# A two-block transformer step in split fp32: the order of the work inside the attention slots, at the front of the second block's first layer, and in its output projections

## The reference, cut to what matters

```python
def first_block(x, ...):                       # one layer
    h = rms_norm(x, norm1_g)
    glu_in, q, k, v, gate_logits = split(h @ w_in)
    a = a_val * sigmoid(a_gate)
    a = silu(rms_norm(causal_depthwise_conv(a, conv_w, conv_b), conv_norm_g))   # 31 taps
    y_a = a @ w_conv_out
    q = rms_norm(q per head) * 64 ** -0.5;  k = rms_norm(k per head)
    o = dilated_window_attention(q, k, v, slopes, ((128, 1), (512, 4), (2048, 16)), mixed by log-sum-exp)
    x = x + (g_a * y_a + g_b * (o @ w_attn_out)) @ w_out       # g = sigmoid(gate_logits + gate_b)
    u = causal_depthwise_conv(rms_norm(x, norm2_g) @ w_up, ffn_conv_w, ffn_conv_b)
    return x + (silu(u_gate) * u_val) @ w_down

def second_block(x, ...):                      # layer a, then layer b
    # a: rope on q and k; an index score selects the 128 best keys of each query; softmax attention over them
    score = einsum(relu(einsum(rope(qi), rope(ki))), wi);  idx = top_k(score, 128)
    y = (softmax_attention(rope(q), rope(k), v, idx) * silu(g)) @ w_out_a
    x = layer_norm(ALPHA * x + y, ln_g[0], ln_b[0])
    # b: stick-breaking attention, no rope
    z = einsum(q, k) * 64 ** -0.5;  before = key < query
    a = exp(log_sigmoid(z) + reverse exclusive cumsum of where(before, log_sigmoid(-z), 0)), 0 elsewhere
    y = ((a @ v) * silu(g)) @ w_out_b
    return layer_norm(ALPHA * x + y, ln_g[1], ln_b[1])
```

## Time and profile before

| | |
|---|---|
| median of 3 runs | 1641.57 us |
| profiled execution | 1639.73 us, span 1637.9 us |
| TensorE (PE) busy | 1516.7 us, 93% of the span |
| VectorE (DVE) busy | 1119.3 us, 68% |
| ScalarE (ACT) busy | 744.4 us, 45% |
| GpSimd (POOL) busy | 365.0 us, 22% |
| mean granted clock of TensorE | 0.968 of full speed |

### The profile page before, as it was taken

The page is one execution under the profiler, slowest core; times in us unless marked ns, Lnnn a source line. Parts: engine busy times, 40 slices in busy tenths (PEclk is TensorE's granted clock), DMA queues, the critical chain, the costliest instruction groups (busy, mean ns, idle before and its releaser), DMA issues.

```text
span 1637.9 us, 19428 instructions
## 1 busy us (share of the span) xinstructions
PE 1516.7 (93%) x6990; PEld 1253.5 (77%) x6990; DVE 1119.3 (68%) x2092; ACT 744.4 (45%) x1464; POOL 365.0 (22%) x293
## 2 busy tenths in 40 slices
PE   8898998889999999999999989978897989999988
PEld 7677887677878788888888777867776868788766
DVE  6836679788955557547737447958787363888966
ACT  6455543556353434334424424345656223556640
POOL 2633346323421111111111113310001112101001
PEclk9999999899999999999999999989999999999999
DMA  6444414451233323333332443364652425555513
GB/s 215 116 136 116 122 52 129 123 148 63 79 115 130 90 90 92 109 97 92 102 93 83 132 123 92 106 169 116 149 141 78 142 103 145 134 128 146 130 54 126
DMA packets 74048, 188.56 MB, mean 115 GB/s; under 512 B 10720, under 2 KB 16224, under 8 KB 73696
## 3 DMA queue, kind: packets, MB, share of 16 engines
q1 hardware_dynamic: 73952, 187.33, 40.2%
...
HBM read 137.48 MB, written 6.29 MB: 88 GB/s over the span
## 4 chain that ended last, share of the span: by engine, by line
PE 62%; DVE 23%; ACT 7%; issue 3%; SPq 3%; DMA 3%; POOL 0%; DVEq 0%; ACTq 0%
PE bank L637 14%; PE bank L638 14%; PE bank L639 14%; PE bank L650 5%; PE bank L651 5%; PE bank L652 5%; DVE bank L1242 3%; SPq L1723 2%; DVE ptl L1178 2%; DVE p L1231 1%; DVE wlo L1168 1%; ACT p L1061 1%; DVE mtab L1290 1%; DVE small L1287 1%; PE bank L677 1%
## 5 line engine op out<-in xcount | busy, mean ns | idle before, releaser
L1647 POOL TENSOR_TENSOR wlo<-raw,whi 128x512 fp32r<-128x512 f32 x241 | 325.3, 1359 | 1200.0 <-ACT whi L880 1199.9
L880 ACT ACTIVATE whi<-raw 128x512 fp32r<-128x512 f32 x466 | 282.8, 622 | 276.6 <-PE bank L639 153.0
L637 PE MATMUL bank<-xh,whi 128*128 128x512 f32 x1000 | 403.0, 403 | 1.3 <-DVE wlo L1168 0.8
L638 PE MATMUL bank<-xl,whi 128*128 128x512 f32 x1000 | 396.3, 396 | 0.0
L639 PE MATMUL bank<-xh,wlo 128*128 128x512 f32 x1000 | 395.4, 395 | 0.0
L639 PEld LDWEIGHTS bank<-xh,wlo 128*128 128x128 f32 x1000 | 191.6, 192 | 42.1
L637 PEld LDWEIGHTS bank<-xh,whi 128*128 128x128 f32 x1000 | 192.6, 193 | 40.8 <-issue 1.4
L638 PEld LDWEIGHTS bank<-xl,whi 128*128 128x128 f32 x1000 | 192.0, 192 | 37.7 <-issue 0.5
L1168 DVE TENSOR_TENSOR wlo<-raw,whi 128x512 fp32r<-128x512 f32 (+1 forms) x225 | 164.2, 739 | 59.5 <-ACT whi L880 41.1
L1242 DVE SCALAR_TENSOR_TENSOR bank<-cbuf,vec,bank 128x512 f32<-128x512 f32 x240 | 164.4, 748 | 18.6 <-ACT bank L905 9.8
L650 PE MATMUL bank<-whi,xh 128*128 128x512 f32 x340 | 136.9, 403 | 9.5 <-DVE xl L1178 7.3
...
## 6 DMA issues: line engine op xcount, KB each, us to landing
...
```

Of the source, the lines that this page charges most:

```text
L637: e.matmul(bank[:, :], h[:, c], a, start=g + i == 0, stop=False)
L638: e.matmul(bank[:, :], h[:, c], b, start=False, stop=False)
L880: e.activation(whi[k % NHL][:, 0:n], raw[u % NRAW][:, c:c + n], ACT.Copy).then_inc(*WHI.tick(k))
L1647: e.tensor_tensor(wlo[k % NHL][:, 0:n], raw[u % NRAW][:, c:c + n], whi[k % NHL][:, 0:n].bitcast(F32), ALU.subtract).then_inc(*WLP.tick(k))
```

## The change

What is changed, in the order of the program:

- First block: `Pq` and `Pk` of the first pair come 5 and 3 plan steps earlier among the value tiles (`PQ0`, `PK0`), those of the fifth pair 3 and 2 steps (`PQ4`, `PK4`). In the slots with preparation, `Pq` stands right behind the scores and `Pk` right behind the transposes; before, both stood in the second half of the slot, one tile step apart. The score banks are used in the order 4, 2, 3 in place of 2, 3, 4. The low parts of the normalised x stand behind the last value tile's low part on DVE.
- Front of layer a: q of pair 0 goes ahead of the value tiles, k of pair 0 into their middle, all later tiles move up, and one half of q of pair 2 is added. The top-k selection runs five of its steps per plan step in place of six.
- Slots of layer a: the rotation is put right behind the scores of a slot; before, it stood behind the transposes. All low parts of weights up to the output projection are made on POOL (`selecting`).
- Slots of layer b: k of a pair, g of the pair before, q of the pair after; before, q, k, g of one pair. q of pair 1 is done before slot 0. Three tile halves stand in each of slots 0 to 9 and two in each of slots 10 to 15; before, three in 0 to 11 and two in 12 to 15. The gate tile 0 was the last of all, and is now in slots 0 and 1.
- First halves of the output projections of a and b: their banks are chosen by what stands in them; the bank of the last gate tile comes fourth, where it was first.

```diff
-FRONT = lambda va1, tiles: (va1[:4] + tiles("q", 0) + va1[4:] + tiles("k", 0) + tiles("g", 0) + tiles("q", 1) + tiles("g", 1)
-                            + tiles("k", 1) + tiles("g", 2) + tiles("g", 3))
+FRONT = lambda va1, tiles: (tiles("q", 0) + va1[:4] + tiles("k", 0) + va1[4:] + tiles("q", 1) + tiles("g", 0)
+                            + tiles("k", 1) + tiles("g", 1) + tiles("g", 2) + tiles("g", 3) + tiles("q", 2)[:1])
-QK_SLOT = [2] * 12 + [0] * 4
+QK_SLOT = [2] * 11 + [1] + [0] * 4
+TOPK_EACH = 5
+PQ0, PK0, PQ4, PK4 = 2, 4, 3, 5
+B_SLOT = [3] * 10 + [2] * 6
-TURN_NOT = "TA"
-SCORE_BANKS = {"": ((2, 3, 4), (2, 3, 4)), ...
+SCORE_BANKS = {"": ((4, 2, 3), (4, 2, 3)), ...
-    return S + c + A + T + list(prep[:1]) + d[:1] + list(prep[1:]) + d[1:]
+    return S + list(prep[:1]) + c + A + T + list(prep[1:]) + d
-    p += v0[:5] + [("Pq", 0)] + v0[5:7] + [("Pk", 0)] + v0[7:]
+    p += v0[:PQ0] + [("Pq", 0)] + v0[PQ0:PK0] + [("Pk", 0)] + v0[PK0:]
-    p += v1[:5] + [("Pq", 4)] + v1[5:7] + [("Pk", 4)] + v1[7:]
+    p += v1[:PQ4] + [("Pq", 4)] + v1[PQ4:PK4] + [("Pk", 4)] + v1[PK4:]
-            c = [half for n in range(1, 6) for half in tiles("qkg", n)]
-            c += tiles("qk", 6) + tiles("qk", 7) + tiles("g", 6) + tiles("g", 7) + tiles("g", 0)
-            size = [3] * 12 + [2, 2, 2, 2]
+            c = []
+            for n in range(1, 6):
+                c += tiles("k", n) + tiles("g", n - 1) + tiles("q", n + 1)
+            c += tiles("k", 6) + tiles("q", 7) + tiles("k", 7) + tiles("g", 5) + tiles("g", 6) + tiles("g", 7)
+            size = B_SLOT
-            p += HALVES("bq", 0) + HALVES("bk", 0) + wide("vb1")
+            p += HALVES("bq", 0) + HALVES("bk", 0) + wide("vb1") + HALVES("bq", 1)
-            bank[x] = 7 if x[1] == 0 else "qk".index(name[1])
+            bank[x] = 4 * (x[1] == 0) + "qk".index(name[1])
+        if x[0] in ("oa0", "ob0"):
+            if x[1] == 0:
+                t, g = "T" + x[0][1], x[0][1] + "g"
+                used = [bank.get((t, 15, u)) for u in range(3)] + [bank[g, 7]]
...
+                ring_o = [b for b in (0, 1, 7, 2, 3, 4, 5) if b not in used][:3] + [bank[g, 7]]
...
+            bank[key] = ring_o[x[1]]
+            continue
-            while t < TURN_US or PLAN[j][0][0] in TURN_NOT:
+            while t < TURN_US or (PLAN[j - 1][0] != "Sa" and ("Sa", 0, 0) in PLAN[:i]) or PLAN[j][0] == "Sa":
-    selecting = range(W.of["va1",][0], W.of[PLAN[PLAN.index(("Sa", 0, 2)) + 1][:2]][0])
+    selecting = range(W.of["va1",][0], W.of["oa0",][0])
-                TOPK_AT[i] = range(j, min(j + 6, 99))
-                j = min(j + 6, 99)
+                TOPK_AT[i] = range(j, min(j + TOPK_EACH, 99))
+                j = min(j + TOPK_EACH, 99)
-            if x in (("v0", 3, 0, 4), ("v0", 3, 4, 8)):      # from ahead of the value tile's low part
-                ... lo_part(XS[kb][1], xr[kb][:, 0:S], XS[kb][0]).then_inc(*DV.tick(("xnl", kb)))
+            if x in (("v0", 3, 0, 4), ("v0", 3, 4, 8)):      # to behind it
+                ... lo_part(XS[kb][1], xr[kb][:, 0:S], XS[kb][0]).then_inc(*DV.tick(("xnl", kb)))
```

15 lines of the change are left out of this document (10 added, 5 removed).

## The result

The changed kernel takes 1602.56 us (median of 4 runs, 1598.48 to 1606.73) against 1641.40 us (1641.11 to 1643.18): a ratio of 0.976, 95% interval 0.973 to 0.979. The forecast was 1590 us with a range of 1570 to 1614 us. The sign and the range held; a quarter of the forecast saving did not come.

A forecast was written before the change was run, and what follows sets the result against it. TensorE, busy 1516.7 of 1637.9 us, was taken as the bound. Savings of 14.6 + 5.8 + 11.5 + 19.7 + 10.0 = 61.6 us, less 10 us for hand-overs, gave 1641.6 - 51.6 = 1590 us, range 1570 to 1614 us.

The forecast's parts named there:

- the 10 us taken off for losses in each slot: Slots of layers a and b: 0.3 us off for each of 32 slots, for imperfect hand-overs, 10 us in all.
- Part 1: First slots of the first block: earlier copies and first scores, no waits of k's transposes for q's bank, 14.6 us saved.
- Part 2: Other slots of the first block: wait partly moved ahead to normalised k, waits for `gb` gone, 5.8 us saved.
- Part 3: Front of layer a: DVE's 7.04 us idle for a swapped tile avoided, TensorE 11.5 us ahead at head 2's scores.
- 2 to 3 us of wait: End of layer a's front: head 0's last score unit still waits this long for the last gate tile.
- The low bound of 5 us: Front of layer a: least saving, if only a 4.3 us bank wait and the wait behind it go.
- Part 4: Slots of layer a: waits for `turnr` copies and slow clock go, 21.7 us less 2 us for POOL's pieces, 19.7 us saved.
- if one in eight of 20 pieces meets such an operation on the path, 2 us: Slots of layer a: cost of POOL's pieces slowing DVE operations through the shared port, bounds none and 18 us.
- Part 5: Slots of layer b and the end: waits for copies and most of that for `ogl` go, 10.0 us saved.
- DVE takes TensorE's place: Rival, layer a: DVE bounds the slots through port lock and rotation ahead of `ptl`, some 20 us lost, 1610 us; chance 0.18.
- The waits of k's transposes: Rival, parts 1 and 2: full waits for normalised k slow the clock each time, 10 us less saved, 1600 us; chance 0.08.
- The rotation's wait for its own copies: Rival, slots of layer a: DVE waits for late swaps, 5.4 us over 12 slots, 65 us, 1655 us; chance 0.04.

The follow-up runs named there:

- the experiment: Changed kernel with the front of layer a in its old order and tile halves one slot back, output wrong: 1631.71 us, ratio 0.9931.
- the short pieces: Changed kernel with POOL's low parts of weights in the slots of layer a cut to 16 of 512 columns: 1595.75 us, ratio 0.9716.
- the rotation by the old rule: Changed kernel with layer a's rotation placed by the old rule, which put it between the first and second masked score: 1631.08 us, ratio 0.9934.

## Why the prediction was right, and where it wasn't

The sign held, and the range held in part by luck. The five parts together were to save 61.6 us, and saved some 23 us less: parts 2, 3 and 4 fell short by about 8 us each. What kept the forecast within 13 us were the 10 us taken off for losses in each slot. In layer b no such losses were seen, and those of layer a had a cause of their own.

**Part 1, first slots: right.** The copies ahead of the first scores were 5 us early, the scores started at 78.4 us where I had 78, the clock stayed at 1.00, and the three waits for the low part of q went. A wait of 1.2 us came at 62 us, as I had it, though of a value tile for q's low part and not of the transposes. Two short ones came that I hadn't, 1.6 us at the first scores and 2.0 us for a bank behind them. 13.4 us against 14.6. (The section on the change has the moves of the transposes wrong: both of the first pair come three steps earlier, both of the fifth pair two. The sums here used three for `Pk` of the first pair.)

**Part 2, slots 8 to 15: no gain.** The new wait for normalised k came, 3.8 us and 0.6 us where I had 4.6, and the waits for `gb` went. The step that failed is the term that I put at nothing: a wait of k's transposes for the low part of q in this stage, and all other copies staying as they were. I checked that k has a tile, output and transposes between it and q in the first slots and carried that over. Slot 8 has neither transposes nor output yet, so k stood one projection behind q in the same bank: 3.6 us. Its copies were late again by 3.0 us at head 10, and small `ptl` waits took the place of those for `gb`. From head 7's scores to head 15's output TensorE is idle for 18.4 us, and before for 19.5 us. Its 825 matmuls keep it busy for 172.1 us, before for 168.7 us:

```profile
195.20:383.40 188.20, 168.74 (x825) 140.18 (x824) 159.40 (x323) 94.15 (x206) 73.96 (x54) 0.96 0.39 107
```

So the waits moved and hardly shrank. The 2.3 us that the table shows as lost are those of the clock in this execution; eleven executions of the new order took 187.6 to 191.7 us against 188.2 us in the one trace of before, and the 5.8 us of the forecast are in none of them.

**Part 3, front of layer a: the mechanism right, the size wrong by 7.6 us.** DVE's idle time of 7.04 us is gone as one wait, and stands there again in pieces: 2.70 us and 1.72 us for swapped tiles, 1.77 us for ACT. The step that failed is the sum of DVE's work that leaves "2 to 3 us of wait" at the last gate tile: 4.9 us came, and TensorE's waits in the front only fell from 9.0 to 7.3 us. I added DVE's work up and took the swaps as landed, since they had been before; but before, DVE was late by its own load, and a swap of 2.44 us of issue and 2.8 us of flight lay behind that. A DVE that is in time meets it. The low bound of 5 us was too high as well: 3.9 us, 4.5 us by the experiment. And the front is not a place where time is kept: 6 us won there by a later rotation cost 5 us two slots on.

**Part 4, slots of layer a: the right waits went, and a new one came that I had the rows for.** The copies from `turnr` are in time (10.9 us of waits gone), the clock is back (6 us), `oa0` gained 1.9 us where I had 2.1. The step that failed is "if one in eight of 20 pieces meets such an operation on the path, 2 us". I let the collisions fall at random, while POOL's pieces are released by ACT at the same place of every slot, and the sum of q's rotation stood there each time: 6 to 7 us on DVE, and 7 us of the time by the short pieces. I had named the rotation as the most exposed and still priced it by chance. That it stood there at all is due to a wait for a tile that DVE doesn't read, which the order of DVE's instructions doesn't show and the code does: 11.9 us of idle time, 8 to 10 us of the time when it is taken away. These two are one loss, not two. The gain from taking 20 pieces off DVE, which I set at about 1 us net, is nothing.

**Part 5, layer b and the end: right, 10.1 against 10.0 us.** The six slots of two halves wait 0.8 to 1.7 us each, 6.8 us for `ptl` where it was 3.1, so 3.8 us where I had 2; the end lost 5.7 of its 6.6 us, where I had 4.2. The two misses cancel. No losses of 0.3 us a slot were seen in the slots of three halves. So the 10 us taken off for hand-overs stood in for losses of another kind: without it the forecast would have been 23 us off and not 13.

**The rivals.** "DVE takes TensorE's place", 1610 us, had the lock, the cause of some 7 of the 23 us by which the parts fell short; the outcome lies between it and the forecast. The waits of k's transposes came, but with a clock of 0.81 and not as 10 us; that its 1600 us lies nearest to the measured time is chance, since other parts made up most of the distance. The rotation's wait for its own copies did not come in the changed kernel's slots, and was shown to be real by one of the two halves of the edit, at 28 us (the rotation by the old rule). The other half is as slow by another way, stack copies that come too late.
